# A two-layer encoder on one core: the second layer's memory keys and values move from the opening to the two layer boundaries, between the transposes of the norms

## What is computed

```
mem_n = rms_norm(mem, g_mem)                      # 256 memory tokens, once
for l in range(2):
    h = rms_norm(x, g_mix[l])
    qa, ka, va, cq, ckv, kr, qm, gates = split(h @ w_in[l])
    y_a = windowed attention(qa, ka, va);  y_b = latent attention(cq, ckv, kr)
    kv = mem_n @ w_mem_kv[l]                      # keys and values of the memory tokens
    y_m = softmax(qm @ keys.T * scale) @ values   # memory attention, 4 heads of 128
    x = x + (sum_i sigmoid(gate_i) * (y_i @ w_branch[l, i])) @ w_out[l]
    h = rms_norm(x, g_ffn[l])
    x = x + swiglu(h)             if l == 0       # dense, width 3584
    x = x + top-2-of-8 experts(h) if l == 1
out = rms_norm(x, g_final)
```

## Time and profile before

| | |
|---|---|
| median of 3 runs | 1835.73 us (1835.28 to 1836.89) |
| profiled execution, span | 1835.7 us |
| TensorE busy | 1770.4 us, 96% |
| VectorE busy | 1389.9 us, 76% |
| ScalarE busy | 1189.7 us, 65% |
| mean granted TensorE clock | 0.985 of full |

### The profile page before, as it was taken

The page is one execution under the profiler, slowest core; times in us unless marked ns, Lnnn a source line. Parts: engine busy times, 40 slices in busy tenths (PEclk is TensorE's granted clock), DMA queues, the critical chain, the costliest instruction groups (busy, mean ns, idle before and its releaser), DMA issues.

```text
span 1835.7 us, 28966 instructions
## 1 busy us (share of the span) xinstructions
PE 1770.4 (96%) x9816; PEld 1519.2 (83%) x9816; DVE 1389.9 (76%) x1506; ACT 1189.7 (65%) x1419; POOL 23.1 (1%) x49
## 2 busy tenths in 40 slices
PE   7999999999998999979999999999999999999997
PEld 6888897899987889868888888888888888888886
DVE  5666574454546664769989989899899899898996
ACT  5465553344434655457877778777777777777775
POOL 2000000000000000000000000000000000000000
PEclk9999998999998999979999999999999999999999
DMA  8544344566655443669989989999999899899990
GB/s 290 164 133 116 119 151 148 166 187 180 187 161 148 127 121 109 227 239 340 373 318 369 370 311 373 347 331 373 338 348 371 314 371 369 305 375 351 332 372 27
DMA packets 213291, 475.01 MB, mean 259 GB/s; under 512 B 14704, under 2 KB 16768, under 8 KB 213232
## 3 DMA queue, kind: packets, MB, share of 16 engines
q1 hardware_dynamic: 212016, 470.61, 74.1%
q0 software_dynamic: 1216, 3.61, 0.6%
HBM read 473.11 MB, written 1.05 MB: 258 GB/s over the span
## 4 chain that ended last, share of the span: by engine, by line
PE 88%; ACT 4%; DVE 4%; issue 3%; DMA 0%; POOL 0%; ACTq 0%; DVEq 0%; POOLq 0%
PE ps L1631 79%; PE ps L1974 2%; PE ps L2007 1%; PE ps L1840 1%; ACT probs L1000 1%; PE ps L1823 1%; ACT whi L865 1%; PE ps L1810 1%; DVE wlo L1169 1%; DVE gates L1187 1%; PE ps L1812 0%; ACT probs L992 0%; PE ps L1894 0%; DMA gain<-in_g_mem 0%; PE ps L1682 0%
## 5 line engine op out<-in xcount | busy, mean ns | idle before, releaser
L1169 DVE TENSOR_TENSOR wlo<-raw,whi 128x1024 fp32r<-128x1024 f32 (+1 forms) x766 | 915.2, 1219 | 326.6 <-ACT whi L865 295.1
L865 ACT ACTIVATE whi<-raw 128x1024 fp32r<-128x1024 f32 (+1 forms) x766 | 796.9, 1055 | 336.3 <-PE ps L1631 333.7
L1631 PE MATMUL ps<-whi,xg_hi 128*128 128x512 f32 x896 | 357.9, 399 | 2.4 <-DVE xg_lo L1175 2.4
L1631 PE MATMUL ps<-wlo,xg_hi 128*128 128x512 f32 x896 | 352.1, 393 | 0.0
L1631 PE MATMUL ps<-whi,xg_lo 128*128 128x512 f32 x896 | 349.9, 391 | 0.0
L1631 PE MATMUL ps<-hT_hi,whi 128*128 128x256 f32 x960 | 277.7, 289 | 6.3 <-ACT gates L875 2.9
L1631 PE MATMUL ps<-hT_lo,whi 128*128 128x256 f32 x960 | 273.4, 285 | 0.0
L1631 PE MATMUL ps<-hT_hi,wlo 128*128 128x256 f32 x960 | 273.0, 284 | 0.0
L1631 PEld LDWEIGHTS ps<-whi,xg_hi 128*128 128x128 f32 x896 | 169.1, 189 | 38.3 <-DVE wlo L1169 5.3
L1631 PEld LDWEIGHTS ps<-wlo,xg_hi 128*128 128x128 f32 x896 | 168.8, 188 | 38.6
L1631 PEld LDWEIGHTS ps<-whi,xg_lo 128*128 128x128 f32 x896 | 169.0, 189 | 35.3
(11 more groups left out here) (299 smaller groups left out, 2120.6 us busy)
## 6 DMA issues: line engine op xcount, KB each, us to landing
raw<-in_w_down_exp SPq DMA_DIRECT2D x200, 512.0 KB, 5.1
raw<-in_w_gate_exp SPq DMA_DIRECT2D x184, 512.0 KB, 5.1
raw<-in_w_up_exp SPq DMA_DIRECT2D x160, 512.0 KB, 5.4
raw<-in_w_in SPq DMA_DIRECT2D x72, 512.0 KB, 3.7
kM<-in_w_up_exp SPq DMA_DIRECT2D x40, 512.0 KB, 5.7
raw<-in_w_gate_dense SPq DMA_DIRECT2D x28, 512.0 KB, 4.2
raw<-in_w_up_dense SPq DMA_DIRECT2D x28, 512.0 KB, 4.1
raw<-in_w_down_dense SPq DMA_DIRECT2D x28, 512.0 KB, 4.3
```

The lines of the kernel that those rows point to most:

```text
L865: s.activation(whi[n % SPLIT][:, 0:w], raw[tile(key)][:, 0:w], ACT.Copy).then_inc(chunk_hi, 1)
L1169: v.tensor_tensor(wlo[n % SPLIT][:, 0:w], raw[tile(key)][:, 0:w], whi[n % SPLIT][:, 0:w].bitcast(F32), ALU.subtract).then_inc(chunk_split, 1)
L1631: ins = mm(o, lhsT, rhs, start=start and i == 0, stop=stop and i == 2, skip_group_check=True)
```

## The change

1. The split memory tokens get tiles of their own, `memT_hi` and `memT_lo` (128x2048 float32 each, 1 MB each), in space that the attention uses too. SyncE writes both to DRAM (`mem_spill`) in the opening, between the last memory chunk and the first chunk of layer 0, and reads both back after the last branch chunk of layer 0. The wait for the writes (`mem_saved`) stands on ScalarE ahead of the copy to `qMT`, on VectorE ahead of the rotary tables, and on SyncE ahead of the reads. 
2. `memk` 1 moves to the first boundary: chunk 0, transposes of tile 0, chunk 1, transposes of tile 1, chunks 2 and 3, then the dense product. `memv` 1 moves to the second boundary in the same pattern, ahead of qa of layer 1. In the opening, the transposes of x stand between chunks 1 and 2 of `memv` 0.
3. The zero matmuls move behind the product `("dense", "GU", 0)` and read a zero tile of the one-pass type.
4. The last down product is done tile 0 in halves, then tile 1 with both halves chunk by chunk.
5. VectorE: a norm is now the means of both tiles, then both multiplies; at the boundaries the mean of tile 0 comes ahead of the last addition to x. The angles of the rotary tables (L1226 to L1245) move in front of `hT_lo` of the first norm of x.

```diff
         chunks / PSUM areas
     transposed(("memT",))
+    psum(("memk", 0), 2, ...); psum(("memv", 0), 3, ...)
     for l in range(DEPTH):
-        psum(("memk", l), 2, ...); psum(("memv", l), 3, ...)
+        if l: psum(("memv", l), 2, ...)
...
+        if l == 0: psum(("memk", 1), 2, full=chunks(mem_chunks("memk", 1)))
         transposed(("hT", 2 * l + 1))
         SyncE
-            for key in opening[SPLIT:] + mixer_chunks(0) + dense_first:
+            for key in opening[SPLIT:]:
+                load(key)
+            sp.wait_ge(hT_split, tl.after("hT_split", ("memT", 3)))
+            for spill, part in zip(mem_spill, memT):
+                sp.dma_start(spill, part).then_inc(mem_saved, 16)
+            for key in mixer_chunks(0):
+                load(key)
+                if key == ("branch", 0, 1, BRANCHES - 1, 1):
+                    wait_full(sp, ("oT", 0, len(units) - 1))
+                    sp.wait_ge(mem_saved, 32)
+                    for spill, part in zip(mem_spill, memT):
+                        sp.dma_start(part, spill).then_inc(mem_back, 16)
+            for key in late_k + dense_first:
                 load(key)
...
-            for key in dense_last + mixer_chunks(1):
+            for key in dense_last + late_v + mixer_chunks(1):
         TensorE
             transposes(("memT",), 0)
+            for c in range(4):
+                wait_piece(("memT",), c)
+                mem_keys(0, c)
             for l in range(DEPTH):
-                stationary_section([("memk", l, c) for c in range(4)], ...)
-                moving_section([("memv", l, c) for c in range(4)], ...)
-            for l in range(DEPTH):
-                transposes(("hT", 2 * l), 2 * l + 1)
+                wait_free(pe, ("memv", l))
+                for c in range(4):
+                    if l == 0 and c == 2:
+                        transposes(("hT", 0), 1)
+                    mem_values(l, c)
+                    if l and c < NT:
+                        transposes(("hT", 2 * l), 2 * l + 1, [c])
...
-                transposes(("hT", 2 * l + 1), 2 * l + 2)
                 if l == 0:
-                    pe.wait_ge(zeros_ready, 1)
-                    (four matmuls of zeros)
+                    pe.wait_ge(mem_back, 32)
+                    wait_free(pe, ("memk", 1))
+                    for c in range(4):
+                        mem_keys(1, c)
+                        if c < NT:
+                            transposes(("hT", 1), 2, [c])
+                else:
+                    transposes(("hT", 2 * l + 1), 2 * l + 2)
...
                     up("dense", 0)
+                    pe.wait_ge(zeros_ready, 1)
+                    (four matmuls of zeros)
```

More of the change, by code:

```diff
@@ L124, in before, with mem_chunks @@
         return self.after(name, key, it) - 1
+def mem_chunks(kind, l):
+    return [(kind, l, c) for c in range(4)]
 def mixer_chunks(l):
@@ L206, in build_tally @@
     transposed(("memT",))
+    psum(("memk", 0), 2, full=chunks(mem_chunks("memk", 0)))
+    psum(("memv", 0), 3, full=chunks(mem_chunks("memv", 0)))
     for l in range(DEPTH):
-        psum(("memk", l), 2, full=chunks([("memk", l, c) for c in range(4)]))
-        psum(("memv", l), 3, full=chunks([("memv", l, c) for c in range(4)]))
-    for l in range(DEPTH):
+        if l:
+            psum(("memv", l), 2, full=chunks(mem_chunks("memv", l)))
         keys = mixer_chunks(l)
@@ L256, in build_tally @@
         tl.add("psum_full3", ("out", l, 1, 0))
+        if l == 0:
+            psum(("memk", 1), 2, full=chunks(mem_chunks("memk", 1)))
         transposed(("hT", 2 * l + 1))
@@ L1438, in _ @@
                                         ALU.add).then_inc(x_added, 1)
-                norm(2 * l + 2, x, normed)
+                        if n and t == 0:
+                            norm_mean(2 * l + 2, 0)
+                norm_apply(2 * l + 2, 0, x, normed)
+                norm_mean(2 * l + 2, 1)
+                if l == 0:
+                    lo_of(late_k[2])
+                norm_apply(2 * l + 2, 1, x, normed)
+                if l == 0:
+                    for key in late_k[3:] + dense_first[0:2]:
+                        lo_of(key)
+                transposed(("hT", 2 * l + 1))
                 if l == 0:
@@ L1923, in _ @@
                     up("dense", 0)
+                    pe.wait_ge(zeros_ready, 1)
+                    for t in range(NT):
+                        wait_free(pe, ("down", t))
+                        for half in range(2):
+                            mm(ps[2 + t][:, 512 * half:512 * (half + 1)], zeros[0:1, 0:P], zeros[0:1, :], start=True,
+                               stop=False, skip_group_check=True)
                     with nc.tensor.Fori(0, DENSE_TURNS) as it:
```

207 lines of the change are left out of this document (110 added, 97 removed).

## The result

The changed kernel takes 1809.26 us (median of 4 runs, 1808.17 to 1810.18), the one before 1836.31 in the runs beside it (1835.28 to 1837.47): ratio 0.9852, 95% interval 0.984 to 0.9864. Forecast: 1809.4 in 1806.5 to 1815. The profiled executions have spans of 1835.7 and 1808.4, so 27.3 us less, where the sum of the prediction said 26.35.

The account below looks back on a forecast made before the run. TensorE, 88% of the chain, was taken to bound the kernel, so only its idle and cold time could go. Terms -24.5 - 0.3 - 2.6 + 2.4 - 0.95 - 0.4 = -26.35 took 1835.7 to 1809.4 us, range 1806.5 to 1815.

Parts of the forecast that it names:

- Opening, first norm included: Opening up to qa: 24.5 us less from moved keys, values and gaps, plus 0.3 less from the first norm's order.
- the angles are what is late next: Opening's end: VectorE's angles run to 40.85, hT_lo's first piece comes about 41.6, TensorE waits 0.4, qa starts about 41.65.
- First boundary: Between out of layer 0 and the dense product: 16.1 us becomes 13.5 with the keys inside, 2.6 less.
- Seeding: Zero matmuls, moved into the 2.45 us wait at the loop's start: cost nothing there, 0.94 without that cover.
- Loop's start: Behind the 2.45 us wait: zero matmuls do not hold the clock, its fall to 0.50 stays, 0 us.
- The first rival: Loop's start (1.5 us) or router (2 us): the clock holds in one or two more places, 1806 to 1808; chance 0.14.
- Second boundary: Last down product to qa of layer 1: 10.9 us becomes 13.3 with values and transposes, 2.4 more.
- Third norm: Ahead of the router: tile 0's multiply starts with the end of the last addition, not 0.97 later; 0.95 us less.
- Last norm: At the end: tile 1's multiply can start when tile 0's ends, about 1830.95 instead of 1831.33; 0.4 us less.
- DRAM copies: Two 1 MB writes in the opening and two reads before layer 0's out loads: taken as 0, with 0 to 5 kept for the range.
- signs of being wrong: Wait for normed at the second boundary, qa or out loads landing late, unexpected half clock; wholly wrong: keys' first chunk awaits DMA.
- Nothing else lies around the span: Base of the sum: the profiled span, 1835.7, equals the runs' median (1835.73) to 0.03 us.

Follow-up runs that it names:

- e2: Changed kernel with ScalarE copying hT_hi before the high parts of qa's chunks 2 and 3, and VectorE's angles behind hT_lo, the values and kvcq's first low parts: 1813.01 us.
- e10: Changed kernel with hT_hi copied before the high parts of qa's chunks 2 and 3, and VectorE's angles before the low part of the values' first chunk: 1807.03 us.
- e12: Changed kernel with hT_hi copied earlier, angles earlier, memory write behind kvcq's chunk 1, and normed tiles split tile by tile behind layer two: 1805.36 us.
- e8: Changed kernel with mean and multiply tile by tile again in the norms and at the first boundary, second boundary's order kept: 1812.14 us.
- e6: Changed kernel with the second layer's memory keys computed in the opening again, the first boundary holding the transposes alone: 1820.58 us.
- e4: Changed kernel with the zero matmuls in plain f32 again, at their new place: 1812.61 us.
- e3: Changed kernel with the four single-pass zero matmuls back ahead of the first dense group: 1813.84 us.
- e11: Changed kernel with hT_hi copied before the high parts of qa's chunks 2 and 3, and the memory's DRAM write issued behind kvcq's chunk 1: 1809.31 us.
- e7: Changed kernel with the memory written to DRAM twice, 4 MB instead of 2 MB, from the same place in SyncE's queue: 1817.02 us.
- e13: The changed kernel once more, with no edit: 1809.33 us median (1807.95 to 1811.2).

## Why the prediction was right

Term by term, each against its column.

- **Opening, first norm included: -24.8 forecast, -23.08 measured** (keys start -1.05, to qa -22.03). The step that failed is "the angles are what is late next". The angles came out as summed (end at 40.47, forecast 40.85). I followed VectorE's program and not ScalarE's, where `hT_hi` stands behind two chunks that wait for TensorE: the wait ahead of qa is 2.46, the sum had 0.4. At a slow beginning ScalarE decides, at a fast one the two tie, and both are gone only in e2, e10 and e12. 0.5 of the difference is the beginning: 20 slow matmuls against 15 before. Against that, the norm's order at its start is worth 0.8 (e8), I had 0.3, and the other 0.27 of "keys start" is the gain vector, by which VectorE's first multiply starts at 8.14 for 8.41. Together this leaves 1.7 us less gain than forecast.
- **First boundary: -2.6 forecast, -3.18 measured.** The order came out as planned: multiply of tile 0 at 267.72, right behind the addition, tile 1's at 270.69, and TensorE without a wait. But the gain is not the keys' alone: about 6 us would have been had without them (e6).
- **Seeding: 0 forecast; the wait covers it, 1.19 us in 2.5.** I had put it at 0.94. In plain f32 it costs 1.2 more (e4), at its old place 2.6 (e3).
- **Loop's start: 0 forecast, -1.46 in the profiled pair.** The first rival came in part. My reason, that zero matmuls do not hold the clock, is borne out by e4; the conclusion, "the fall stays", is not: the clock fell there in 4 of 12. That this profile is one of the eight is luck.
- **Second boundary: +2.4 forecast, +2.1 measured** (0.66 in the table, with the clock's 1.46 added; against the profiles where it fell, 276.05, it is +2.14). The slack of 0.4 held: tile 1's multiply ended at 529.47, its transposes began at 529.95.
- **Third norm: -0.95 forecast, -1.12 measured**, -1.05 by e8 alone. (By its own rows the 0.97 in that step is 291.82 - 290.91 = 0.91.) The stretch behind it, to the gather, is 0.47 shorter too, which is within what the clock does there: 14.67 to 16.25 in kernels with the same order.
- **Last norm: -0.4 forecast, nothing measured.** The last multiply starts 4.3 us before the end in both kernels. Tile 1's mean now stands ahead of tile 0's multiply and waits for ScalarE's last squares, so the first tile loses what the second wins.
- **DRAM copies: 0 forecast, 0 to 0.6 measured** (e11). One of the prediction's signs of being wrong did show: ScalarE waited 2.14 us for the load of qa's first chunk. The write landed in 12.6 and 14.5 us, the reads in 6.4 and 9.4, and no TensorE wait stands in front of the keys. The slack was smaller than I thought: one more write costs 6.7 us (e7).
- **The base.** "Nothing else lies around the span" is wrong: every run's time is its own span and 1.7 to 1.8 us (1810.18 for 1808.4). It was hidden because the median of the before runs stood near the span of the profiled one. That 1.8 too low and the 0.95 too high of the sum, with the profile's place in the spread, offset each other: the 0.1 us between forecast and median is luck. The terms miss by up to 1.7 us (opening) and 1.5 (loop's start), with opposite signs, and their sum by 0.95 for that reason.

## What to carry to other kernels

Independent work that is moved into a wait is worth the wait only so far as nothing cheaper would have shortened it: here some 6 of the 14.7 us that the first boundary gave back came from reordering the norm and taking zero matmuls out of cold time. When work leaves a stretch, write down the new order of every engine there, ScalarE's with its buffer waits too; two engines that tie for the end hide each other, so take both away in one experiment. Compare two kernels of this size by lengths between the same instructions and not by times alone, since four executions of one program spread over 3 us (e13), and the clock alone made up to 2.1 us of difference in the opening and 1.5 behind the loop's start.

## What the runs showed of the hardware that I had not expected

- The first 15 to 23 key matmuls of 256 columns started 0.213 us apart in 6 of 14 profiles (before, changed, e3, e6, e8, e13), the pace at the recorded 0.50 elsewhere (1.2 GHz), and 0.12 apart in 8. The trace's first clock record is the rise to 1.00: it stands at 17.6 to 19.5 us in the six, where the pace changes, and at 12.6 to 14.3 in the eight. Ahead of that rise there is no record, and the profile's column prints 1.00 where it has none, as from 14 to 18 us of the changed kernel. So its 1.00 at the start of a program means nothing; the distance of matmuls shows the pace. The slow beginning costs up to 2.1 us.
- Behind the loop's start the clock fell in some profiles and stayed up in others with the same program there, with 1.3 us of idle time behind 1.2 of seeding (e2 fell, e13 did not). The Trainium skill, TensorE: Matmul & The Clock Gate (Part 1, What's actually happening), has activity release the throttle; one-row matmuls without a gap neither raised the clock here (7.19 us at 0.50 in the kernel before) nor kept it from falling (3.70 us, then 0.53, e4).
- Two writes of 1 MB among loads, all together at 397 to 410 GB/s (20 to 35 us), landed in 12.6 and 14.5 us, and in 7.8 and 9.5 with fewer loads around them (e11).
